# Feed-forward in chunks of 6, 8 and 8 hidden tiles, the down products of two chunks as 2x2 block products, and one more weight sum made by an accumulating transfer

## The chip, the cores and the metric

The kernel runs on one core of a Trainium2 chip, in one launch. The metric is the device time of one execution in microseconds (us). All arithmetic is on fp32 data.

## The reference

One layer of a hybrid encoder trunk runs over 512 prompt frames and 32 sample frames with the same weights (D_MODEL 1024, D_FF 2816, 544 columns of tokens in all):

```python
def swiglu(x, wg, wu, wd):
    return (jax.nn.silu(x @ wg) * (x @ wu)) @ wd
...
    x = x + 0.5 * swiglu(rms_norm(x, g_ffn1), w_ffn1_gate, w_ffn1_up, w_ffn1_down)
    y, st = hybrid_mixer(rms_norm(x, g_mix), pos, C, n, m, R, w_in, b_gates, g_gn_mlstm, g_gn_ret, w_out)
    x = x + y
    x = x + 0.5 * swiglu(rms_norm(x, g_ffn2), w_ffn2_gate, w_ffn2_up, w_ffn2_down)
```

`hybrid_mixer` projects with `w_in` (4104 columns), runs four mLSTM heads and four retention heads, and projects back with `w_out`. A last RMSNorm over the 1024 features gives the two outputs `y_prompt` and `y_sample`; the states go out too. The change touches the two feed-forward networks (FFN1 and FFN2) and their ends.

## The kernel before

The residual stream stays in SBUF transposed as `xT`: 8 tiles of 128 features by 544 tokens. An fp32 product is made of three passes of TensorE over split operands: `w_hi*x_hi + w_hi*x_lo + w_lo*x_hi`. ACT makes each `hi` by a copy that rounds, DVE each `lo` by subtracting. A matmul here is a 128x128 weight tile against 272 tokens, half of the 544.

**A feed-forward** has 22 hidden tiles of 128. The first four ("plain") are ordinary gate and up products over 8 k-tiles. The other 18 are made in "pairs" of two tiles, by a 2x2 block scheme of Winograd's kind (the features halved one way, the tokens the other): 7 block products in place of 8. A pair has a gate step (e=0, banks `dense[0]` and one of `core_banks`) and an up step (e=1). One step is 7 products `o` = 0 to 6 of 4 k-tiles by 3 passes: 84 matmuls. Products 0, 2, 4 and 6 use bank 0 of the step, 1 and 5 bank 1, 3 bank 2; products 0, 1 and 3 start a bank, and the others add to what is in it. So before the next product goes into a bank, its state is read out, where the output needs it apart: ACT copies products 0, 1, 2 and 4 into `kept` (`KEPT`, `copy_product` L1137), and DVE builds the gate and up values of the four quarters from these copies and the banks (`gate_first`, `gate_second`, `gate_third`, `up_first`, `up_second`, `up_third`, `up_last`). The product after a copy waits for `product_copied`.

The weights of the seven products are blocks of 128x512: 0, 1, 3, 4 and 5 are loaded by SyncE's queue. Blocks 1 and 4 then get a second quarter of the weights added by a transfer with accumulation that GpSimd (POOL) issues (`add_blocks` L2130). Block 2 is a sum that DVE makes of two blocks (`sum_t2`), block 6 likewise (`sum_t4` L1529, the addition at L1534). While step g runs, ACT and DVE prepare the `hi` (`block_to_hi` L1106) and the `lo` (`block_to_lo` L1536) of step g+1's blocks, each in the slot that the same product of step g has just left: `hi` of block o waits for `product_done` of product o.

The pairs come in two chunks, pairs 0 to 7 and 8 to 17 (`PAIRS`). The hidden tiles of a chunk (12, then 10) are then multiplied by `w_down` in ordinary products (`down` L779, `product` L614): 22 k-tiles by 8 output tiles by 3 passes by 2 token halves are 1056 matmuls for each feed-forward. DVE adds each finished tile to `xT` (L1798). In chunk 1 the squares of `xT` for the next norm follow on DVE, and POOL adds them up in SBUF (`add_square` L2120). The last tile of FFN2 goes out in two parts (`last_tile` L808), with the column sums (L836), the transposes (L845) and the scaling of the output (L1839) behind them.

The order on each engine is that of the code, written out by hand for five engines; semaphores are all that ties them together. SyncE's queue and POOL's queue are in order too.

Of the kernel before, what the change touches and what calls it, by code (L numbers as in the profile page):

```python
# [12 lines left out]
P = 128  # L13
# [31 lines left out]
def hybrid_trunk_step(nc, x_prompt, x_sample, state_mlstm_C, state_mlstm_n, state_mlstm_m, state_ret_R,  # L45
# [29 lines left out]
    U_DOWN = [[u + 2 * STD + 2 * DT * c for c in range(2)] for u in U_STD]  # L75
# [12 lines left out]
    LAST_COLS = [slice(2 * P, T), slice(0, 2 * P)]  # L88


    END_CHUNKS = [(2, 3, NC), (0,), (1,)]
    END_COLS = [slice(2 * P, T), slice(0, P), slice(P, 2 * P)]
    STEP_OF = {c: step for step, chunks in enumerate(END_CHUNKS) for c in chunks}
    DVE_COLS, ACT_COLS = slice(0, 5 * P), slice(5 * P, D)
    RAW = 4
# [6 lines left out]
    T_DOWN = [[t + 2 * STD + DT * c for c in range(2)] for t in T_STD]  # L102

    def down_unit(s):

        for n in range(2):
            for c in range(2):
                if U_DOWN[n][c] <= s < U_DOWN[n][c] + 2 * DT:
                    return n, c, s - U_DOWN[n][c]
        return None  # L110

    def k_tiles(s):

# [11 lines left out]
    NEGATED = (2, 6)  # L125
    KEPT = (0, 1, 2, 4)
# [8 lines left out]
    def units_before(n, c):  # L135

        return U_STD[n] + 2 * STD if c == 0 else U_DOWN[n][0] + 2 * DT

    with ExitStack() as ctx:
# [37 lines left out]
        rms_bias = sb("rms_bias", [P, NC + 1])  # L177
# [2091 lines left out]
```

## Time and profile before

| | before |
|---|---|
| median of 3 runs | 1064.79 us (1064.61 to 1065.61) |
| span of the profiled execution | 1063.2 us |
| its own time | 1063.2 us, 1.6 us under the median |
| PE (TensorE matmul) busy | 1055.5 us, 99% |
| DVE, ACT, POOL busy | 64%, 44%, 18% |
| granted TensorE clock | 9 tenths or more in each of 40 slices |

PE is busy nearly all of the span; a busy PE is one that has a matmul under way, and neighbouring matmuls overlap, so the duration of one is longer than the distance between two.

### The profile page before, as it was taken

How to read it: one execution, taken by the hardware profiler on the slowest of the kernel's cores; microseconds unless marked ns; L12 is line 12 of the kernel's file. 1: busy time of each engine (PE TensorE's matmuls, PEld its weight loads, DVE VectorE, ACT ScalarE, POOL GpSimd, SP SyncE). 2: the span in 40 equal slices, each digit the busy share in tenths (PEclk: the TensorE clock that was granted, in tenths of full speed). 3: DMA queues.
4: the chain of work that ended last, by engine and by line, in shares of the span. 5: the costliest groups of instructions: out<-in, count | busy, mean ns of one | idle time of the engine just before them, and what ended most of it. 6: DMA issues, size and time to landing. Idle time of an engine off the chain costs nothing.

```text
span 1063.2 us, 20510 instructions
## 1 busy us (share of the span) xinstructions
PE 1055.5 (99%) x8425; PEld 1052.1 (99%) x8425; DVE 684.2 (64%) x1170; ACT 465.7 (44%) x822; POOL 189.8 (18%) x169
## 2 busy tenths in 40 slices
PE   9999999999999999999999999999999999999997
PEld 8999999999999999999999999999999999999997
DVE  6997752367866676655655556598875236777555
ACT  6466641256652345433222224446664114666323
POOL 1122100112201211210332222212210002220111
PEclk9999999999999999999999999999999999999999
DMA  8589482479833377445454224547958328892422
GB/s 225 121 172 200 100 196 84 96 159 177 176 82 96 64 135 139 71 68 80 69 80 75 67 78 62 140 91 170 206 110 187 92 82 166 178 180 52 124 75 84
DMA packets 245493, 127.84 MB, mean 120 GB/s; under 512 B 9228, under 2 KB 243892, under 8 KB 245272
## 3 DMA queue, kind: packets, MB, share of 16 engines
q1 hardware_dynamic: 207032, 106.79, 41.6%
q0 software_dynamic: 38288, 19.72, 14.6%
q8 instruction: 67, 1.10, 0.4%
q14 instruction: 26, 0.21, 0.1%
q10 hardware_dynamic: 80, 0.02, 0.0%
HBM read 123.22 MB, written 3.29 MB: 119 GB/s over the span
## 4 chain that ended last, share of the span: by engine, by line
PE 98%; DMA 1%; DVE 0%; SPq 0%; issue 0%; ACT 0%
PE dense L623 52%; PE dense L768 31%; PE core_banks L768 5%; PE core_banks L623 3%; PE dense L691 1%; PE core_banks L928 1%; PE core_banks L943 1%; PE dense L824 1%; PE core_banks L946 1%; PE core_banks L918 1%; DMA x_tok<-in_x_prompt 1%; PE core_banks L955 0%; PE core_banks L912 0%; PE core_banks L914 0%; PE core_banks L805 0%; PE core_banks L666 0%
## 5 line engine op out<-in xcount | busy, mean ns | idle before, releaser
L1481 DVE TENSOR_TENSOR w_lo<-w_raw,w_hi 128x1024 fp32r<-128x1024 f32 (+2 forms) x118 | 131.7, 1133 | 55.1 <-ACT w_hi L1068 55.0
L1068 ACT ACTIVATE w_hi<-w_raw 128x1024 fp32r<-128x1024 f32 (+2 forms) x118 | 105.2, 904 | 89.3 <-PE dense L623 81.4
L623 PE MATMUL dense<-h_hi,w_hi 128*128 128x272 f32 x684 | 142.5, 290 | 0.0
L623 PE MATMUL dense<-xg_hi,w_hi 128*128 128x272 f32 x672 | 142.2, 293 | 0.0
L623 PE MATMUL dense<-h_lo,w_hi 128*128 128x272 f32 x684 | 141.1, 287 | 0.0
L623 PE MATMUL dense<-h_hi,w_lo 128*128 128x272 f32 x684 | 140.9, 287 | 0.0
L623 PE MATMUL dense<-xg_lo,w_hi 128*128 128x272 f32 x672 | 138.9, 288 | 0.0
L623 PE MATMUL dense<-xg_hi,w_lo 128*128 128x272 f32 x672 | 138.8, 287 | 0.0
L768 PE MATMUL dense<-x_op_hi,w_lo 128*128 128x272 f32 x432 | 124.6, 289 | 0.0
L768 PE MATMUL dense<-x_op_hi,w_hi 128*128 128x272 f32 x432 | 124.5, 288 | 0.0
L768 PE MATMUL dense<-x_late_hi,w_lo 128*128 128x272 f32 x432 | 124.5, 288 | 0.0
L768 PE MATMUL dense<-x_late_hi,w_hi 128*128 128x272 f32 x432 | 124.3, 288 | 0.0
L768 PE MATMUL dense<-x_late_lo,w_hi 128*128 128x272 f32 x432 | 124.2, 287 | 0.0
L768 PE MATMUL dense<-x_op_lo,w_hi 128*128 128x272 f32 x432 | 124.0, 287 | 0.0
L1539 DVE TENSOR_TENSOR w_lo<-w_src,w_hi 128x512 fp32r<-128x512 f32 x126 | 85.9, 690 | 50.1 <-ACT w_hi L1120 49.9
L1798 DVE SCALAR_TENSOR_TENSOR xT<-dense,xT 128x544 f32<-128x544 f32 x38 | 27.5, 724 | 135.4 <-PE dense L623 135.4
L623 PEld LDWEIGHTS dense<-h_lo,w_hi 128*128 128x128 f32 x684 | 107.8, 188 | 0.0
L623 PEld LDWEIGHTS dense<-h_hi,w_lo 128*128 128x128 f32 x684 | 106.8, 188 | 0.0
L623 PEld LDWEIGHTS dense<-h_hi,w_hi 128*128 128x128 f32 x684 | 106.7, 188 | 0.1
L623 PEld LDWEIGHTS dense<-xg_lo,w_hi 128*128 128x128 f32 x672 | 105.8, 188 | 0.0
L623 PEld LDWEIGHTS dense<-xg_hi,w_lo 128*128 128x128 f32 x672 | 105.1, 188 | 0.0
L623 PEld LDWEIGHTS dense<-xg_hi,w_hi 128*128 128x128 f32 x672 | 104.7, 188 | 0.2
(341 smaller groups left out, 2212.1 us busy)
## 6 DMA issues: line engine op xcount, KB each, us to landing
w_raw<-in_w_ffn_up SPq DMA_DIRECT2D x91, 256.0 KB, 3.6
w_src<-in_w_ffn_gate SPq DMA_DIRECT2D x90, 256.0 KB, 4.6
w_raw<-in_w_in SPq DMA_DIRECT2D x32, 512.0 KB, 8.9
w_raw<-in_w_ffn_down SPq DMA_DIRECT2D x32, 384.0 KB, 4.0
w_raw<-in_w_ffn_down SPq DMA_DIRECT2D x32, 320.0 KB, 3.5
w_src<-in_w_ffn_gate POOLq DMA_DIRECT2D x36, 256.0 KB, 5.2
w_raw<-in_w_ffn_up POOLq DMA_DIRECT2D x36, 256.0 KB, 5.8
w_raw<-in_w_out SPq DMA_DIRECT2D x8, 512.0 KB, 3.9
```

The source lines that it names most:

```text
L623: last = nc.tensor.matmul(out[:, half, 0:TH], w[:, s % 4, k, :], x(kt)[:, half * TH:(half + 1) * TH], start=start and n == 0 and m == 0, s ...
L691: last = nc.tensor.matmul(bank_of(u)[:, half, 0:TH], w[:, u, k, :], x(k)[:, half * TH:(half + 1) * TH], start=part == "hh" and k == 0, sto ...
L768: last = nc.tensor.matmul(banks[BANK[o]], w[:, k, :], x[:, k, :], start=o in OPENS and k == 0 and m == 0, stop=k == KH - 1 and m == 2, ski ...
L824: last = nc.tensor.matmul(bank_of(t)[:, part, 0:cols.stop - cols.start], w[:, (s + u) % 4, kt - u * split, :], x[:, kt, cols], start=kt == ...
L918: nc.tensor.matmul(X[:, 3, CH[c]], p(h, 1, CH[c]), p(h, 0, CH[c]), start=True, stop=True)
L928: last = nc.tensor.matmul(X[:, b, o * V1:(o + 1) * V1], k_tail[:, c, :], v_tok[:, c, :], start=True, stop=True)
L943: last = nc.tensor.matmul(out, score_tail[:, block], v_tok[:, c, :], start=True, stop=c == 0)
L946: last = nc.tensor.matmul(out, sum_ident[:, block], state, start=False, stop=True)
L1068: nc.scalar.activation(w_hi[:, s % 4, 0:k_tiles(s), :], raw, ACT.Copy).then_inc(w_hi_ready, 1)
L1481: nc.vector.tensor_tensor(w_lo[:, s % 4, 0:nk, :], w_raw[:, s % RAW, 0:nk, :], w_hi[:, s % 4, 0:nk, :].bitcast(F32), ALU.subtract).then_in ...
L1539: nc.vector.tensor_tensor(block_of(w_lo, n, o), source(p % 2, o), block_of(w_hi, n, o).bitcast(F32), ALU.subtract)\
L1798: nc.vector.scalar_tensor_tensor(x, halves(tile), factor, x, ALU.mult, ALU.add).then_inc(evicted, 1)
```

## The change

The hidden tiles are now worked in three chunks: 6 (the four plain ones and pairs 0 and 1), 8 and 8 tiles. Only the first chunk's down products are still ordinary (`down(n)`, 6 k-tiles). Those of the other two chunks are made in four steps each, `down_pair(n, c, d)` for d = 0 to 3: a step makes two output tiles over eight hidden tiles, again by 7 block products of 4 k-tiles by 3 passes, with weight blocks of `w_down` that are loaded, summed and split as those of a pair. There are now 26 steps for each feed-forward. Their moving operands are seven combinations of four hidden half tiles, which DVE and ACT prepare for each group of two tiles: four sums (`sum_h`), seven `hi` (`h_to_hi`) and seven `lo` (`h_to_lo`) of 128x272 each. DVE adds every one of the 7 products to `xT` (`take_down`).

Two things change for the pair steps. ACT copies products 0, 1 and 2 only; of product 4 DVE itself reads the bank (`gate_second`, `up_second`), and product 6 waits for that. And DVE's `sum_t4` is gone: a third accumulating transfer of POOL's adds a quarter of the weights to block 2, once block 2's `lo` is made (`add_last_block`), and that is block 6.

At the end of a feed-forward the squares of tiles 1 to 5 are made by ACT (`square_end`) and added by transfers from SBUF to SBUF with accumulation, one after the other (`add_end_square`); those of the last two tiles are added by DVE. The end of FFN2 is rewritten for tiles that come out in pairs.

```diff
-    PAIRS = (range(0, 8), range(8, 18))
-    FC, F0 = (12, FT - 12), (0, 12)
...
+    PAIRS = (range(0, 2), range(2, 10), range(10, 18))
+    FC, F0 = (STD + 2, 8, 8), (0, STD + 2, STD + 10)
...
-    KEPT = (0, 1, 2, 4)
+    COPIED = (0, 1, 2)
+
+
+    DOWNS = DT // 2
+    STEPS = NP + 2 * DOWNS
...
+    FIRST_ORDER = (0, 1, 3, 2, 4, 5, 6)
+    LAST_ORDER = (0, 1, 3, 2, 5, 4, 6)
...
                     if o == 6:
-                        pe.wait_ge(product_copied, 4 * P_ + 4)
+                        if e == 0:
+                            pe.wait_ge(pair_gate_made, 3 * Q + 2)
+                        else:
+                            pe.wait_ge(pair_up_taken, 3 * Q + 2)
...
+            def down_pair(n, c, d):
...
+                    pe.wait_ge(down_taken, BLOCKS * D + 2)
+                    pe.wait_ge(block_lo, BLOCKS * g + 6)
+                    part(5, range(KH // 2))
+                    pe.wait_ge(down_taken, BLOCKS * D + 4)
+                    pe.wait_ge(h_op_lo_ready, lo_made(n, k, 4))
+                    part(4, range(KH)).then_inc(product_done, 1)
...
+                for rank, o in enumerate(order_of(g)):
...
+                    before = {2: 0, 4: 2, 5: 1, 6: 4}
+                    if o in before:
+                        pe.wait_ge(down_taken, BLOCKS * D + order_of(g).index(before[o]) + 1)
...
             def gate_second(n, p):
-                dve.wait_ge(product_copied, 4 * pair_index(n, p) + 4)
-                nc.vector.tensor_tensor(pair_gate[1][:, TH:T], kept[:, 0, 3, :], kept[:, 0, 1, :], ALU.add).then_inc(pair_gate_made, 1)
+                dve.wait_ge(product_done, done_by(step_of_pair(n, p), 4))
+                dve.wait_ge(product_copied, 3 * pair_index(n, p) + 2)
+                out = pair_gate[1][:, TH:T]
+                nc.vector.tensor_tensor(out, pair_banks(0)[0], out, ALU.subtract).then_inc(pair_gate_made, 1)
...
-            def sum_t4(n, p):
...
+            def take_down(n, c, d, o):
...
+                dve.wait_ge(product_done, done_by(g, o))
...
+                x = xT[:, 2 * d + m, half * TH:(half + 1) * TH]
+                nc.vector.scalar_tensor_tensor(x, pair_banks(g % 2)[BANK[o]], factor, x, ALU.mult, ALU.add).then_inc(down_taken, 1)
...
+            def add_end_square(n, j):
+
+                pool.wait_ge(end_squared, DT * n + j + 1)
+                if j > 1:
+                    pool.wait_ge(end_landed, 16 * ((DT - 3) * n + j - 1))
+                nc.gpsimd.dma_start(sq_sum[:, :], sq[:, :], accum_op=ALU.add).then_inc(end_landed, 16)
...
+            def add_last_block(g, quarter):
+
+                e = g % 2
+                pool.wait_ge(block_lo, BLOCKS * g + 3)
+                nc.gpsimd.dma_start(source(e, 6), quarter(1, 0), accum_op=ALU.add).then_inc(block_summed[e][6], 16)
```

In DVE's program, around products 4 and 5 of a gate step of FFN1, the order before was this. `w_lo` is a weight block's `lo` for the next step, `sq` and `rstd` hold the gate values, `h_lo` the split of hidden values, L1589 is `gate_second`.

```order
L1539 TENSOR_TENSOR w_lo<-w_raw,w_hi 128x512 [waits block_hi]
L1585 TENSOR_TENSOR sq<-core_banks,kept 128x272 [waits product_copied,product_done,pair_h_made]
L1637 TENSOR_TENSOR h_lo<-sum_ident,h_hi 128x544 [waits pair_h_hi]
L1539 TENSOR_TENSOR w_lo<-w_raw,w_hi 128x512 [waits block_hi]
L1589 TENSOR_TENSOR rstd<-kept 128x272 [waits product_copied]
L1539 TENSOR_TENSOR w_lo<-w_raw,w_hi 128x512 [waits block_hi]
L1593 SCALAR_TENSOR_TENSOR rstd<-dense,kept 128x272 [waits product_done]
L1637 TENSOR_TENSOR h_lo<-h_f,h_hi 128x544 [waits pair_h_hi]
```

At the same place of the changed program (L1717 is `block_to_lo`, L1759 `h_to_lo`, L1792 `gate_second`):

```order
L1717 TENSOR_TENSOR w_lo<-w_raw,w_hi 128x512 [waits block_hi]
L1759 TENSOR_TENSOR h_op<-h_raw,h_op 128x272 [waits h_op_hi_ready]
L1786 TENSOR_TENSOR sq<-core_banks,sq 128x272 [waits product_copied,product_done]
L1717 TENSOR_TENSOR w_lo<-w_raw,w_hi 128x512 [waits block_hi]
L1759 TENSOR_TENSOR h_op<-h_raw,h_op 128x272 [waits h_summed,h_op_hi_ready]
L1792 TENSOR_TENSOR rstd<-dense,rstd 128x272 [waits product_copied,product_done]
L1717 TENSOR_TENSOR w_lo<-w_raw,w_hi 128x512 [waits block_hi]
L1759 TENSOR_TENSOR h_op<-h_raw,h_op 128x272 [waits h_op_hi_ready]
L1798 TENSOR_TENSOR rstd<-dense,rstd 128x272 [waits product_copied,product_done]
L1717 TENSOR_TENSOR w_lo<-w_raw,w_hi 128x512 [waits block_hi]
```

`gate_second` stands behind the `lo` of block 4 and an operand's `lo` now as it stood behind the `lo` of block 4 before, but it reads the bank, and it needs product 4 itself where it needed ACT's copy.

In PE's program the first matmul of product 6 of a gate step waited before for the block's `lo` and for ACT's copy:

```order
L768 MATMUL dense<-x_late_hi,w_hi 128x272
L768 MATMUL dense<-x_late_lo,w_hi 128x272
L768 MATMUL dense<-x_late_hi,w_lo 128x272
L768 MATMUL dense<-x_late_hi,w_hi 128x272 [waits block_lo,product_copied]
L768 MATMUL dense<-x_late_lo,w_hi 128x272
```

In the changed program it waits for the `lo` and for DVE's `gate_second`:

```order
L853 MATMUL dense<-x_late_hi,w_hi 128x272
L853 MATMUL dense<-x_late_lo,w_hi 128x272
L853 MATMUL dense<-x_late_hi,w_lo 128x272
L853 MATMUL dense<-x_late_hi,w_hi 128x272 [waits block_lo,pair_gate_made]
L853 MATMUL dense<-x_late_lo,w_hi 128x272
```

Nothing else stands between product 5 and product 6 in either.

The third place is DVE's program at the start of a chunk's down products. Before, it was this (L1637 and L1624 finish the last pair's hidden values, L1481 is the `lo` of a `w_down` tile, L1798 the addition of a finished tile to `xT`):

```order
L1624 TENSOR_TENSOR sum_ident<-sum_ident,rstd 128x544 [waits pair_gate_silu,pair_up_taken]
L1630 SCALAR_TENSOR_TENSOR h_f<-dense,sq 128x272 [waits pair_gate_silu,product_done]
L1637 TENSOR_TENSOR h_lo<-sum_ident,h_hi 128x544 [waits pair_h_hi]
L1637 TENSOR_TENSOR h_lo<-h_f,h_hi 128x544 [waits pair_h_hi]
L1481 TENSOR_TENSOR w_lo<-w_raw,w_hi 128x768 [waits w_hi_ready] x2
L1798 SCALAR_TENSOR_TENSOR xT<-dense,xT 128x544 [waits unit_done]
L1481 TENSOR_TENSOR w_lo<-w_raw,w_hi 128x768 [waits w_hi_ready] x2
L1798 SCALAR_TENSOR_TENSOR xT<-dense,xT 128x544 [waits unit_done]
```

In the changed program the first down step, d=0, begins so (L1747 and L1756 or L1759 make the last group's operands, L1712 is `sum_t2`, L1846 `take_down`):

```order
L1846 SCALAR_TENSOR_TENSOR xT<-dense,xT 128x272 [waits product_done]
L1759 TENSOR_TENSOR h_op<-h_raw,h_op 128x272 [waits h_summed,h_op_hi_ready]
L1846 SCALAR_TENSOR_TENSOR xT<-dense,xT 128x272 [waits product_done]
L1846 SCALAR_TENSOR_TENSOR xT<-core_banks,xT 128x272 [waits down_taken,product_done]
L1759 TENSOR_TENSOR h_op<-h_raw,h_op 128x272 [waits h_summed,h_op_hi_ready]
L1717 TENSOR_TENSOR w_lo<-w_src,w_hi 128x512 [waits block_hi]
L1712 TENSOR_TENSOR w_raw<-w_raw 128x512 [waits block_lo,block_loaded1_5,block_summed1_1]
L1756 SCALAR_TENSOR_TENSOR h_op<-h_raw,h_op 128x272 [waits h_op_hi_ready]
L1717 TENSOR_TENSOR w_lo<-w_raw,w_hi 128x512 [waits block_hi]
L1846 SCALAR_TENSOR_TENSOR xT<-dense,xT 128x272 [waits product_done]
L1717 TENSOR_TENSOR w_lo<-w_raw,w_hi 128x512 [waits block_hi] x3
L1846 SCALAR_TENSOR_TENSOR xT<-dense,xT 128x272 [waits down_taken,product_done]
```

Between two evictions stand now the last group's `lo` operands and the weight blocks of the next step, and an eviction comes for each block product.

## Rows read from the trace of the kernel before

**Rows 1.** The page's head, its engines, and the chain that ended last

```profile
span 1063.2 us, 20510 instructions
...
PE 1055.5 (99%) x8425; PEld 1052.1 (99%) x8425; DVE 684.2 (64%) x1170; ACT 465.7 (44%) x822; POOL 189.8 (18%) x169
...
PE 98%; DMA 1%; DVE 0%; SPq 0%; issue 0%; ACT 0%
```

**Rows 2.** PE's waits: what for, us in total, times, longest

```profile
PE core_banks L866 <- POOL ones L2111: 1.1, 1, 1.1
```

**Rows 3.** Windows, a pair stretch, then a down stretch: length, busy time of each engine (count), clock, DMA share, GB/s

```profile
740.00:760.00 20.00, 20.00 (x162) 20.00 (x161) 17.84 (x33) 12.36 (x25) 5.12 (x4) 1.00 1.01 218
820.00:840.00 20.00, 20.00 (x161) 20.00 (x161) 4.92 (x6) 3.47 (x5) 0.00 (x0) 1.00 0.53 130
```

**Rows 4.** Groups of instructions: the costliest of the down products, busy, mean ns, idle before

```profile
L623 PE MATMUL dense<-h_hi,w_hi 128*128 128x272 f32 x684 | 142.5, 290 | 0.0
```

**Rows 5.** Timeline, gate step: product 4's last, product 6's first matmul, and ACT and DVE between

```profile
956.31 0.29 PE L768 MATMUL dense<-x_late_hi,w_lo 128*128 128x272 f32 x1
...
956.63 0.40 ACT L1141 ACTIVATE kept<-dense 128x272 f32<-128x272 f32 x1 [0.26 <-PE dense L768]
...
956.93 0.63 ACT L1120 ACTIVATE w_hi<-w_raw 128x512 fp32r<-128x512 f32 x1
...
957.59 0.69 DVE L1539 TENSOR_TENSOR w_lo<-w_raw,w_hi 128x512 fp32r<-128x512 f32 x1
...
957.94 0.28 PE L768 MATMUL dense<-x_late_hi,w_hi 128*128 128x272 f32 x1
```

**Rows 6.** Timeline, DVE's queue in the up step behind it

```profile
968.72 0.43 DVE L1610 TENSOR_TENSOR h_f<-h_f,sq 128x272 f32<-128x272 f32 x1
969.08 0.43 DVE L1614 TENSOR_TENSOR sum_ident<-kept 128x272 f32<-128x272 f32 x1
969.43 0.68 DVE L1539 TENSOR_TENSOR w_lo<-w_src,w_hi 128x512 fp32r<-128x512 f32 x1
970.03 0.43 DVE L1618 SCALAR_TENSOR_TENSOR sum_ident<-dense,kept 128x272 f32<-128x272 f32 x1
```

**Rows 7.** Timeline, ACT's copy of the same product in two steps that follow each other

```profile
961.15 0.40 ACT L1141 ACTIVATE kept<-dense 128x272 f32<-128x272 f32 x1 [0.49 <-PE dense L768]
...
971.67 0.40 ACT L1141 ACTIVATE kept<-dense 128x272 f32<-128x272 f32 x1 [0.81 <-PE dense L768]
```

**Rows 8.** Timeline, PE's restart behind a DVE result

```profile
1052.80 0.46 DVE L1812 TENSOR_TENSOR sq<-sq,sum_ident 128x288 f32<-128x288 f32 x1
...
1053.35 0.35 PE L836 MATMUL dense<-ones,sq 128*128 128x1 f32 x2
```

**Rows 9.** One line's transfers: L2138, accumulating, 256 KB, into block 4

```profile
L2138 POOL DMA_DIRECT2D w_src<-in_w_ffn_gate x18: 1270/1279/1296, 37.4 to 951.0; - x18
...
DMA to landing us min/median/max: 4.5/5.3/8.3
```

**Rows 10.** One line's transfers: L2207, plain, 272 KB, from POOL's queue

```profile
L2207 POOL DMA_DIRECT2D row_all<-row_copy x3: 547/591/614, 410.2 to 449.0; - x3
...
DMA to landing us min/median/max: 3.6/3.7/8.3
```

**Rows 11.** Groups of instructions by form, of the seams: busy, mean ns, idle before

```profile
L1486 DVE SCALAR_TENSOR_TENSOR xg_lo<-xT,gains,xg_hi 128x544 fp32r<-128x544 f32 x24 | 27.6, 1168 | 4.5 <-ACT xg_hi L1080 4.1
L1624 DVE TENSOR_TENSOR sum_ident<-sum_ident,rstd 128x544 f32<-128x544 f32 x18 | 13.0, 720 | 0.1
L1080 ACT ACTIVATE xg_hi<-xT,gains 128x544 fp32r<-128x544 f32 x24 | 17.5, 746 | 60.2 <-DVE xT L1798 59.6 <-DVE xT L1848 0.6
L1074 ACT ACTIVATE sq<-xT 128x544 f32<-128x544 f32 x8 | 5.2, 646 | 1.5 <-POOL sum_ident L2128 1.5
L2128 POOL TENSOR_TENSOR sum_ident<-sum_ident,sq 128x544 f32<-128x544 f32 x22 | 31.6, 1436 | 121.5 <-DVE sq L1786 89.6 <-ACT sq L1074 31.9
```

**Rows 12.** The end: the last product matmul, the last scaling, and the last window

```profile
1056.11 0.28 PE L824 MATMUL dense<-h_hi,w_lo 128*128 128x256 f32 x1
...
1059.06 0.55 DVE L1839 TENSOR_SCALAR y_tok<-y_tok,rms_tok 128x640 f32<-128x640 f32 x1
...
1058.00:1063.00 5.00, 0.33 (x2) 0.14 (x1) 1.54 (x6) 1.45 (x4) 0.00 (x0) 0.68 0.82 317
```

**Rows 13.** The page's DMA queues: packets, MB, share of 16 engines

```profile
q1 hardware_dynamic: 207032, 106.79, 41.6%
q0 software_dynamic: 38288, 19.72, 14.6%
```

More of the change, by code:

```diff
@@ L85, in hybrid_trunk_step @@
     X_BY_DVE = [piece for piece in X_PIECES if piece != X_BY_ACT]
[L88 to L93, printed above, removed]
+    HALF_COLS = [slice(0, TH), slice(TH, T)]
+    END_CHUNKS = [(0, 1), (2, 3, NC)]
+    END_COLS = [slice(0, 2 * P), slice(2 * P, T)]
     DVE_COLS, ACT_COLS = slice(0, 5 * P), slice(5 * P, D)
+    Y_PARTS = (2, 2, 2, 2, 1)
     RAW = 4
@@ L761, in pair @@
                     if p == 0:
                         pe.wait_ge(x_op_ready, BLOCKS * n + o + 1)
[L763 to L764 removed]
+                    pe.wait_ge(block_lo, BLOCKS * g + o + 1)
                     x_hi, x_lo = x_op(x_op_hi, x_late_hi, o), x_op(x_op_lo, x_late_lo, o)
[L766 to L769 removed]
@@ L832, in column_sums @@
-            def column_sums(out, source, chunks):
-                for c in chunks:
-                    n = P if c < NC else TS
-                    last = nc.tensor.matmul(out[0:n, c:c + 1], source[:, CH[c]], ones[:, 0:1], start=True, stop=True)
-                return last
-            def turn_last(step):
-                pe.wait_ge(out_taken, DT - 1 if step == 2 else DT - 2)
-                pe.wait_ge(x_gained, DT + step)
-                j = DT - 1
-                for c in END_CHUNKS[step]:
-                    last = nc.tensor.transpose(last_turn(c), x_gain[:, j % 2, CH[c]], ident[:, :])
+                    nc.tensor.transpose(X[:, 2 + j % 2, CH[c]], x_gain[:, j % 2, CH[c]], ident[:, :])
@@ L859, in turn_dummies @@
+                for c in END_CHUNKS[step]:
+                    last = nc.tensor.matmul(final_sum(c), sq_last[:, 0, CH[c]], ones[:, 0:1], start=True, stop=True)
+                last.then_inc(final_sums, 1)
             def turn_dummies(n):
@@ new lines, in ffn, with sum_t2 @@
+                pair(n, 0, 1)
+                up_last(n, 1, NP // 2 * n)
+                first_to_lo(n, STD + 1)
+                first_to_lo(n, STD)
+                down(n)
+                block_to_lo(n, STEPS * n + STEP_DOWN + 1, BLOCKS - 1)
+                for c in (1, 2):
+                    for p in PAIRS[c]:
+                        pair(n, c, p)
+                    for d in range(DOWNS):
+                        down_pair(n, c, d)
+            def sum_t2(g):
+                e = g % 2
+                dve.wait_ge(block_summed[e][1], 16 * (g // 2 + 1))
+                dve.wait_ge(block_loaded[e][5], 16 * (g // 2 + 1))
+                if g > 1:
+                    dve.wait_ge(block_lo, BLOCKS * (g - 1))
+                nc.vector.tensor_tensor(source(e, 2), source(e, 1), source(e, 5), ALU.add).then_inc(pair_summed, 1)
@@ L1666, in pair @@
                     if o == 0:
-                        if e == 0 and p - 2 in PAIRS[c]:
+                        if deferred and e == 0:
                             up_last(n, p - 1, Q - 1)
-                        if more:
-                            sum_t2(n, p + 1)
-                    if o == 3 and more:
-                        sum_t4(n, p + 1)
+                        if follows_blocks(g):
+                            sum_t2(g + 1)
+                    if deferred:
+                        for h_o in ((), (1,), (2,), (4, 5), (), (), ())[o] if e == 0 else ():
+                            sum_h(n, k, h_o)
+                        for h_o in (((), (), (), (), (0,), (1,), (3,)), ((2,), (4,), (5,), (6,), (), (), ()))[e][o]:
+                            h_to_lo(n, k, h_o)
```

1143 lines of the change are left out of this document (664 added, 479 removed).

## The prediction

> **What bounds the kernel now.** I read the page's head and its chain first. PE is busy 1055.5 of 1063.2 us, and 98% of the chain that ended last is PE [rows 1]. PE's own waits are four in all and the longest is 1.1 us, at the start of the mixer [rows 2]. So nothing can be won but matmuls, and every wait put in front of a matmul costs its full length. The windows show what lies beside PE: in a pair stretch DVE is busy 17.84 of 20 us, ACT 12.36, and the DMA engines' share is 1.01; in a down stretch DVE is busy only 4.92 us and the share is 0.53 [rows 3]. The change takes matmuls out of the idle stretches and turns them into more of the crowded kind.
>
> **1. The matmuls.** The h rows are three kinds of 684 [rows 4], with the 60 of the last tile 2112 down matmuls for both networks. A down stretch has 161 in 20 us, 124.2 ns each [rows 3]. A pair step of 84 lasts from 961.15 to 971.67, 10.52 us, 125.2 ns each [rows 7]. After the change 2 x 6 x 8 x 3 x 2 = 576 stay plain, and 2 x 8 x 84 = 1344 are block products. −2112 x 0.1242 + 576 x 0.1242 + 1344 x 0.1252 = −262.3 + 71.5 + 168.3 = **−22.5 us**. This is the whole gain: the kept copies of product 4 and `sum_t4` leave engines that PE didn't wait for.
>
> **2. Product 6 of a pair step.** Before, product 4 ends at 956.60 and product 6 starts at 957.94 [rows 5]: 1.34 us, product 5's length, without a gap, since ACT's copy (0.40 us, from 956.63) was long done. Now product 6 waits for `gate_second` or `up_second`, and DVE does it behind the next step's block 4 `lo`, which itself waits for a `hi` that ACT can start only when product 4 is done. From the end of product 4: hand-over 0.03, `hi` 0.63, hand-over 0.03 [rows 5], so the `lo` starts at 0.69. DVE's queue then moves by 0.60 for a 512-wide `lo` (969.43 to 970.03) and 0.36 for a 272-wide operation (968.72 to 969.08) [rows 6]; in a gate step an `h_to_lo` is next, in an up step `up_first_gated`, both 272 wide. So the sum starts at 0.69 + 0.60 + 0.36 = 1.65 and ends 0.43 later, at 2.08. PE starts about 0.09 after DVE's end (1053.26 to 1053.35) [rows 8]: 2.17 against 1.34, **0.83 us of idle PE**. It occurs in the 16 pairs of the last two chunks of each network, 32 steps, less 0.36 in the four that have no operand's `lo` between (the first gate step of a chunk). Pairs 0 and 1 have no such `lo` ahead. 28 x 0.83 + 4 x 0.47 = **+25.1 us**. Below, 0.75 a step if the hand-overs are shorter (+22); above, 0.95 if DVE comes late to the `lo` (+30), as its queue is nearly full. Nothing hides it, since PE has no other work in its queue.
>
> **3. The first down step of a chunk (4 of them).** Here the last group's hidden values are only finished after the last pair step. I walk DVE's queue from the end of that step, t = 0. PE does the old k-tiles of products 0, 1 and 3 first (27 matmuls), then the last ones (9), product 2 (12), half of 5 (6): product 4 could start after 54 matmuls, at 6.6. It waits for `take_down` of product 2. Take 3 can start at 4.65 (36 matmuls and the pipeline); behind it stand an `h_lo` (0.36), a weight `lo` (0.60), `sum_t2` (0.60), an `h_lo` (0.36), a weight `lo` (0.60), by the pitches of [rows 6], so take 2 starts at 7.5 and PE at 8.05. That is 1.5 us, **+6** (3 to 8).
>
> **4. Block 6 behind that step.** In the same queue the `lo` of block 2 of the next step comes at 8.5 and ends at 9.2. Only then POOL may issue the transfer that makes block 6. An accumulating 256 KB transfer of this kind lands 5.3 us after its issue (4.5 to 8.3) [rows 9]: 14.5. `hi` 0.63 and `lo` 0.60 with hand-overs follow, to 15.8, and only behind this `lo` stands take 0 of the next step, 0.43. PE's product 2 of that step waits for take 0: 16.3 against 14.8. **+6** for four (3 to 10, with the landing). In the steps after that the loop from block 2's `lo` to product 2 of the next step adds up to 1.4 + 0.1 + 5.3 + 0.7 + 0.6 + 0.4 + 0.2 = 8.7 us, where 72 matmuls give 9.0: hidden, by 0.3 us. A landing later than the median shows, so I put **+1** (0 to 5) for late ones.
>
> **5. FFN1 to mixer.** The five transfers of squares run one after the other; each link is a square on ACT (0.65), a hand-over (0.1) and a landing. No row has an accumulating 272 KB transfer within SBUF; a plain one from POOL's queue takes 3.7 [rows 10], an accumulating one 5.3 [rows 9]. I take 4.7 between them, nearer to the one that accumulates: 5.45 a link. POOL's queue lets the first go about 0.9 us before step d=2, so the fifth lands at −0.9 + 4.7 + 4 x 5.45 = 25.6 after that step's start, 15.1 after the last step's, which itself ends at 10.5. Behind it stand a square 0.65, `add_end` 0.72, `normed_lo` 1.17, take 0.43, `normed_hi` 0.75, `normed_lo` 1.17, `add_end` 0.72, with hand-overs some 6 us [rows 11], where PE waits for the sums. They are ready at 21, the first mixer product at 21.9. By the matmuls alone it would start at 10.5 + 32 x 0.124 + 0.6 = 15.1. **+7** (3 to 10). Before, POOL's additions took 1.44 each [rows 11].
>
> **6. The end of FFN2.** Product 6 of the last step stands behind `sum_last(0)`, which needs the fifth landing: PE goes on at 15.7 where 72 matmuls and the transposes end at 9.6: +6. Then the tail. Before, 3.2 us lie between the last product's end (1056.39) and the end of the last scaling (1059.61) [rows 12]; now an addition, three reads of transposes and all five scalings stand behind it, 5.3 us as I add them, +2. **+8** (4 to 12).
>
> **Sum.** −22.5 + 25.1 + 6 + 6 + 1 + 7 + 8 = +30.6, 1063.2 + 30.6 = 1093.8. The profiled execution is 1.6 us under the median of 1064.8, so against the median 1095.4; I say **1096**. All terms at their low ends give 1077, all at the high ones 1118.
>
> **Rivals.**
> *(a) The DMA engines become the bound* (0.14). POOL's queue took 14.6% of 1063.2 us for 19.72 MB [rows 13], and 72 weight transfers make nearly all of that: 2.1 us of all 16 engines each; SyncE's took 41.6% for 106.79 MB, 1.09 us for 256 KB. A step had 5 x 1.09 + 2 x 2.1 = 9.7 us and gets 11.8, more than the 10.5 of its matmuls and about 0.5 more than a step with its stalls. Against it: the times of packets include their waiting for each other. For it: the 1.01 of [rows 3]. Over 52 steps, half of the full 0.5, 14 us: about 1110, in the range.
> *(b) Part of the waits are not there* (0.08): DVE or ACT are given earlier starts than I walked, the squares' transfers land in 3.7 us. With terms 3 to 6 at half and term 2 at 0.6 us a step (19): 1063 − 22.5 + 19 + 14 + 1.6 = 1076; 1066 to 1077.
> *(c) The other side: product 6 doesn't wait* (0.08). One mechanism would do it: if `gate_second` ran as soon as product 4 is done, 0.03 + 0.43 + 0.09 = 0.55, well before 1.34, term 2 is nothing and the kernel takes 1070; with the seams at their low ends (3 + 3 + 3 + 4) 1057. It decides where the stall falls under 22.5/32 = 0.7 us a step with the seams free. For it speaks only that DVE's order could have been read wrongly; the order shows the `lo` ahead of it.
> *(d) The clock* (0.08). In the last window, where PE has 0.33 us of work in 5, the granted clock is 0.68, and it is 1.00 in both busy stretches [rows 12, 3]. In the seams PE now idles some us at a time. If it falls to the lower level behind each of the two seams, 50 matmuls at twice 0.124 cost 6 us: 1102, in the range. The Trainium skill (TensorE: Matmul & The Clock Gate, Part 1: The HAM clock gate) says that the array is throttled to half its clock unless recent activity releases it. The trace agrees in so far as the clock sank where PE stopped.
>
> **How the numbers follow.** Forecast 0.62, (a) 0.14, (b) 0.08, (c) 0.08, (d) 0.08. From 1076 to 1118 lie the forecast, (d), most of (a) and the top of (b). Under 0.2% (2 us) a run can't be told from no change. Only (c) without most of the seams is faster, 0.07, or the same, 0.02; the rest is slower, 0.91.
>
> **What would show it.** Term 1: 192 fewer matmuls (their records may be a few short). Term 2: PE's waits name DVE's `gate_second` (L1792) and `up_second` (L1816) about 16 times each, at 0.7 to 0.9 us; this one decides, and if they are absent I am wrong by 25 us. Terms 3 and 4: eight waits for `take_down` (L1846) of 1 to 2 us, one pair to each chunk. Term 5: one wait of some 6 us for the sums of squares ahead of the mixer, with transfers of 272 KB that land 4 to 5 us after their issue. Term 6: the same ahead of the last product 6, and a tail of 5 us. (a): waits that name DMAs of weights, a share above 1.0 in down steps; (d): a granted clock under 1.0 behind a seam. It would be wrong, too, if landings of the third transfer stretch well over 5.3 us, since the loop of term 4 has 0.3 us to spare: each us more costs up to 40 us over the steps, which is the largest single risk above the range.

## The result, and the profile after

The changed kernel takes 1149.97 us (median of 4 runs, 1143.43 to 1153.29) against 1064.74 us before: 1.079 times as long, 95% interval 1.075 to 1.082. The prediction was 1096 us with a range of 1076 to 1118. The sign was right, the size was not: +85 us where +31 were forecast.

The page's head after the change, then PE's longest waits (what for, us in total, times, longest):

```profile
span 1150.2 us, 20921 instructions
...
PE 1058.8 (92%) x8229; PEld 1041.4 (91%) x8229; DVE 759.7 (66%) x1441; ACT 509.6 (44%) x943; POOL 286.5 (25%) x246
...
PE 71%; DMA 13%; DVE 7%; ACT 4%; issue 4%; SPq 0%; POOL 0%; DVEq 0%; ACTq 0%; POOLq 0%
```

```profile
PE dense L853 <- DVE xT L1846: 16.1, 8, 2.9
PE dense L853 <- DVE rstd L1792: 14.2, 18, 2.1
PE dense L739 <- DVE xg_lo L1673: 11.7, 1, 11.7
PE dense L739 <- DVE w_hi L1663: 11.6, 1, 11.6
PE dense L853 <- DVE h_raw L1816: 11.3, 16, 0.7
PE dense L853 <- ACT sq L1293: 5.0, 2, 2.8
PE core_banks L977 <- ACT x_gain L1411: 2.8, 2, 1.4
PE core_banks L986 <- DVE y_tok L1688: 1.9, 1, 1.9
...
PE core_banks L774 <- DVE sum_ident L1993: 1.3, 1, 1.3
...
PE dense L986 <- ACT x_gain L1451: 0.4, 1, 0.4
```

PE was 99% busy and 98% of the chain [rows 1]; it is now 92% and 71%. To see where the time went, the root of the norm sums is a mark that both kernels have once behind FFN1 and once ahead of FFN2. Before (first and last start):

```profile
L1089 ACT ACTIVATE rstd<-core_banks,eps x2: 715/716/718, 387.2 to 685.7; 128x544 f32<-128x544 f32 x2
```

After:

```profile
L1233 ACT ACTIVATE rstd<-core_banks,eps x2: 713/716/718, 441.0 to 739.4; 128x544 f32<-128x544 f32 x2
```

| | before | after |
|---|---|---|
| FFN1, to the root | 387.2 | 441.0 (+53.8) |
| mixer | 298.5 | 298.4 |
| FFN2, to the end | 377.5 | 410.8 (+33.3) |

So nothing happened in the mixer, and FFN1 lost 20 us more than FFN2. The windows say where: first a pair stretch, then the first two down steps of FFN1's last chunk, then two at the seam to the mixer (columns as in [rows 3]).

```profile
200.00:220.00 20.00, 18.59 (x146) 18.15 (x145) 16.56 (x36) 12.38 (x29) 6.66 (x6) 1.00 1.00 196
360.00:380.00 20.00, 15.70 (x111) 15.26 (x110) 14.20 (x32) 8.35 (x17) 5.13 (x4) 0.92 0.78 142
400.00:420.00 20.00, 8.44 (x63) 8.22 (x62) 3.73 (x10) 2.93 (x6) 2.88 (x5) 0.77 0.63 83
420.00:440.00 20.00, 7.04 (x28) 6.16 (x27) 5.25 (x7) 4.08 (x5) 3.47 (x14) 0.59 0.66 153
```

Where PE had been idle for some us, the granted clock sank too: 0.59 at the seam means that most of that window's records ran at the lower of the two levels.

In a pair step the predicted wait stands as it was walked. The timeline of one gate step: the last matmul of product 4, ACT's and DVE's operations behind it, the last matmul of product 5 and the first two of product 6; the next step's product 6 follows.

```profile
902.28 0.29 PE L853 MATMUL dense<-x_late_hi,w_lo 128*128 128x272 f32 x1
...
902.66 0.63 ACT L1265 ACTIVATE w_hi<-w_raw 128x512 fp32r<-128x512 f32 x1 [0.55 <-PE dense L853]
...
903.20 0.74 ACT L1301 ACTIVATE h_op<-h_raw 128x272 fp32r<-128x272 f32 x2
903.33 0.69 DVE L1717 TENSOR_TENSOR w_lo<-w_raw,w_hi 128x512 fp32r<-128x512 f32 x1
...
903.78 0.29 PE L853 MATMUL dense<-x_late_hi,w_lo 128*128 128x272 f32 x1
903.94 0.43 DVE L1759 TENSOR_TENSOR h_op<-h_raw,h_op 128x272 fp32r<-128x272 f32 x1
...
904.29 0.43 DVE L1792 TENSOR_TENSOR rstd<-dense,rstd 128x272 f32<-128x272 f32 x1
...
904.78 0.40 PE L853 MATMUL dense<-x_late_hi,w_hi 128*128 128x272 f32 x1 [0.71 <-DVE rstd L1792]
...
905.01 0.29 PE L853 MATMUL dense<-x_late_lo,w_hi 128*128 128x272 f32 x1
...
916.28 0.39 PE L853 MATMUL dense<-x_late_hi,w_hi 128*128 128x272 f32 x1 [0.71 <-DVE h_raw L1816]
```

The block's `lo`, the operand's `lo` and the sum follow at 0.61 and 0.35 us, and PE starts 0.06 us after the sum's end. From one product 6 to the next are 11.50 us where a step took 10.52 [rows 7]: 0.98 us. 0.71 of them are named as a wait. This wait is counted from the end of the matmul before, which lasts 0.29 us where the distance between two is 0.125, so product 6 starts 0.87 us late; and its second matmul comes 0.23 us behind the first, another 0.10.

At the seam, ACT and POOL stand still for 17 us, and DVE behind them for 13.8, until a transfer of squares lands. SyncE's queue (SPq) has issued three 512 KB loads of `w_in` ahead of it:

```profile
398.99 0.99 SPq L624 DMA_DIRECT2D w_raw<-in_w_in  x2
...
400.03 3.65 SPq L624 DMA_DIRECT2D w_raw<-in_w_in  x1
400.62 0.85 POOL L2398 DMA_DIRECT2D sum_ident<-sq  x1
...
417.50 0.66 ACT L1404 ACTIVATE sq<-xT 128x544 f32<-128x544 f32 x1 [17.04 <-DMA sum_ident<-sq]
418.06 0.33 ACT L1194 ACTIVATE w_hi<-w_gates 128x32 fp32r<-128x32 f32 x2
...
418.42 0.29 DVE L1663 TENSOR_TENSOR w_hi<-w_gates,w_hi 128x32 fp32r<-128x32 f32 x2 [13.76 <-ACT w_hi L1194]
418.45 0.86 POOL L2398 DMA_DIRECT2D sum_ident<-sq  x1 [16.97 <-ACT sq L1404]
418.75 0.37 SPq L624 DMA_DIRECT2D w_raw<-in_w_in  x1
418.77 0.82 PE L739 MATMUL dense<-xg_hi,w_hi 128*128 128x272 f32 x2 [11.56 <-DVE w_hi L1663]
```

This is the fourth of FFN1's five transfers and takes 16.9 us; the fifth, issued at 418.45, takes 15.5. The landings of all ten such transfers (L2398), and of the third accumulating weight transfer (L2412), min, median, max:

```profile
DMA to landing us min/median/max: 3.3/3.3/16.9
...
DMA to landing us min/median/max: 4.4/5.7/8.0
```

### The profile page after: what moved, and what is told of

It is laid out like the page before. It is cut to its first block, busy times and chain, and to the rows that moved or that the text cites. A ratio compares the mean times of both kernels' runs of the same rounds, so it can differ in the third digit from the quotient of the medians.

```text
span 1150.2 us, 20921 instructions
## 1 busy us (share of the span) xinstructions
PE 1058.8 (92%) x8229; PEld 1041.4 (91%) x8229; DVE 759.7 (66%) x1441; ACT 509.6 (44%) x943; POOL 286.5 (25%) x246
## 4 chain that ended last, share of the span: by engine, by line
PE 71%; DMA 13%; DVE 7%; ACT 4%; issue 4%; SPq 0%; POOL 0%; DVEq 0%; ACTq 0%; POOLq 0%
PE dense L729 29%; PE dense L853 27%; PE core_banks L853 6%; DMA sum_ident<-sq 3%; DMA w_raw<-in_w_ffn_up 3%; DMA w_raw<-in_w_ffn_down 3%; PE core_banks L729 3%; DMA w_src<-in_w_ffn_gate 3%; ACT w_hi L1265 2%; DVE w_lo L1717 2%; PE dense L799 1%; PE core_banks L1080 1%; PE core_banks L1065 1%; DMA x_tok<-in_x_prompt 1%; PE core_banks L1055 1%
## 5 line engine op out<-in xcount | busy, mean ns | idle before, releaser
L1717 DVE TENSOR_TENSOR w_lo<-w_raw,w_hi 128x512 fp32r<-128x512 f32 x182 | 123.8, 688 | 79.2 <-ACT w_hi L1265 77.0
L1265 ACT ACTIVATE w_hi<-w_raw 128x512 fp32r<-128x512 f32 x182 | 112.8, 629 | 134.8 <-DMA w_raw<-in_w_ffn_up 47.2
L1265 ACT ACTIVATE w_hi<-w_src 128x512 fp32r<-128x512 f32 x182 | 112.5, 627 | 135.1 <-DMA w_src<-in_w_ffn_gate 49.5
L1717 DVE TENSOR_TENSOR w_lo<-w_src,w_hi 128x512 fp32r<-128x512 f32 x182 | 124.4, 689 | 65.3 <-ACT w_hi L1265 62.7
L853 PE MATMUL dense<-h_op,w_hi 128*128 128x272 f32 x768 | 150.1, 294 | 16.1 <-DVE xT L1846 16.1
L853 PE MATMUL dense<-x_late_hi,w_hi 128*128 128x272 f32 x432 | 128.2, 297 | 26.3 <-DVE rstd L1792 14.2
L853 PEld LDWEIGHTS dense<-h_op,w_hi 128*128 128x128 f32 x768 | 121.8, 191 | 18.5 <-DVE xT L1846 18.3
L1668 DVE TENSOR_TENSOR w_lo<-w_raw,w_hi 128x1024 fp32r<-128x1024 f32 (+1 forms) x70 | 87.5, 1250 | 43.5 <-ACT w_hi L1211 43.3
L853 PE MATMUL dense<-h_op,w_lo 128*128 128x272 f32 x384 | 112.1, 292 | 0.0
L853 PEld LDWEIGHTS dense<-x_late_hi,w_hi 128*128 128x128 f32 x432 | 81.1, 188 | 34.0 <-DVE rstd L1792 18.2
L853 PEld LDWEIGHTS dense<-x_op_hi,w_hi 128*128 128x128 f32 x432 | 81.5, 189 | 8.9 <-ACT sq L1293 5.7
```

Source lines behind the costliest of these rows:

```text
L853: last = nc.tensor.matmul(out, w[:, k, :], x, start=o in OPENS and k == 0 and m == 0, stop=k == KH - 1 and m == 2, skip_group_check=o not ...
L1265: nc.scalar.activation(block_of(w_hi, n, o), source(e, o), ACT.Copy).then_inc(block_hi, 1)
L1668: nc.vector.tensor_tensor(w_lo[:, s % 4, 0:nk, :], w_raw[:, s % RAW, 0:nk, :], w_hi[:, s % 4, 0:nk, :].bitcast(F32), ALU.subtract).then_in ...
L1717: nc.vector.tensor_tensor(block_of(w_lo, n, o), source(g % 2, o), block_of(w_hi, n, o).bitcast(F32), ALU.subtract)\
```

## The experiments

Each kernel was timed beside the kernel before (1064.9 to 1065.1 us in these rounds). The changed kernel took 1149.97.

| edit | us | ratio to before, 95% |
|---|---|---|
| sums first | 1143.77 | 1.072 to 1.075 |
| squares by POOL | 1132.15 | 1.061 to 1.064 |
| late w_in | 1139.84 | 1.067 to 1.075 |
| block 6 by DVE | 1132.49 | 1.062 to 1.065 |
| sums first, block 6 by DVE | 1105.38 | 1.034 to 1.041 |
| sums first, squares, early take | 1123.70 | 1.050 to 1.057 |
| all four | 1095.22 | 1.024 to 1.032 |
| and w_in split last | 1092.89 | 1.021 to 1.029 |
| and better DVE order | 1074.03 | 1.007 to 1.010 |
| and root first | 1069.88 | 1.004 to 1.006 |
| better order, block 6 by transfer | 1132.15 | 1.060 to 1.066 |
| before, sum from the bank | 1101.89 | 1.033 to 1.036 |
| before, block 6 by transfer | 1095.13 | 1.027 to 1.033 |
| before, both | 1101.05 | 1.033 to 1.036 |

**Sums first.** DVE does the sum for product 6 ahead of the next block's `lo`.

```diff
                         if e == 0:
                             gate_first(n, p, Q)
+                            gate_second(n, p)
                         else:
                             up_first(n, p)
-                    if o == 5:
-                        if e == 0:
-                            gate_second(n, p)
-                        else:
+                            up_first_gated(p, Q)
                             up_second(n, p)
...
-                    if e and o == 4:
-                        up_first_gated(p, Q)
```

> DVE does gate_second and up_second ahead of the next step's block 4 lo; nothing else is changed. Theory A (each pair step idles at product 6 only because DVE's sum stands behind that lo): the 32 waits of PE for these sums, 0.7 us each with a restart of 0.1, fall away and a step goes back from 11.5 to 10.5 us, 28 to 31 us in all, so about 1120 us. Rival B (the DMA engines, at a share of 0.95 to 1.0 in these stretches, set the step's length anyway): the waits turn into waits for weight blocks, the step stays above 11 us, gain under 12 us, about 1140.

The waits at product 6 of a steady step are gone (two, in the first gate step of each network, are left), but 6 us are all that came of it. The new waits are at product 2, for ACT's copy of product 0, and those for `take_down` rose from 16.1 to 20.2 us:

```profile
PE dense L853 <- DVE xT L1846: 20.2, 10, 3.9
...
PE dense L853 <- ACT h_raw L1293: 9.4, 13, 1.6
PE dense L853 <- ACT sq L1293: 4.7, 4, 2.0
PE dense L853 <- DVE rstd L1792: 4.1, 2, 2.1
```

The gain is as small as rival B had it, but its sign, waits for weight blocks, isn't there: PE waits for ACT's copies. Another limit of almost the same length stood behind the first. Which one, the next runs tell.

**Squares by POOL's addition.** `add_end_square` adds with an instruction.

```diff
-                nc.gpsimd.dma_start(sq_sum[:, :], sq[:, :], accum_op=ALU.add).then_inc(end_landed, 16)
+                nc.gpsimd.tensor_tensor(sq_sum[:, :], sq_sum[:, :], sq[:, :], ALU.add).then_inc(end_landed, 16)
```

> The five squares of each network's end are added by POOL's own tensor addition in place of the accumulating transfer. Theory A (two of the transfers ahead of the mixer take 16.9 us because they lie behind the 512 KB loads of w_in in the DMA engines): the two idle stretches of PE ahead of the mixer, 11.6 and 11.7 us, go down to under 3 us together, and with the clock kept up the kernel gains 22 to 28 us, about 1124. Rival B (the mixer's weights themselves land late): PE waits for w_in instead, gain under 10 us, about 1142.

It gave 18 us, less than theory A's 22 to 28. The first of the two long waits is gone, the second is 6.0 us; there ACT waits 9.88 us for the landing of a `w_in` tile, which stands in its program ahead of the last squares. So theory A holds for the greater part and rival B for the rest.

**The squares' transfers kept, w_in held back.** SyncE waits for the last of them ahead of three loads; its queue is in order, so all that it issues later waits too.

```diff
                     sp.wait_ge(block_lo, BLOCKS * STEP_LAST + (2, BLOCKS, 6, 6)[s % RAW])
+                    sp.wait_ge(end_landed, 16 * (DT - 3))
```

> The transfers of squares are kept, but the first three loads of w_in are held back until the last of them has landed. Theory A: all five transfers of FFN1 land in 3.3 to 3.6 us instead of two in 16.9; PE's wait moves to the weights of the mixer, which now come some 10 us after the squares; gain 5 to 15 us, 1135 to 1145. Rival C (the transfer is slow for a reason of its own, as what ACT and DVE write or read beside it): two still take above 10 us and the kernel gets slower, 1160.

```profile
DMA to landing us min/median/max: 3.3/3.3/3.6
```

All ten transfers now land in 3.3 to 3.6 us, and PE has one wait of 15.2 us left at this place instead of two of 11.6 and 11.7. The 16.9 and 15.5 us were time beside what SyncE's queue had under way, the 512 KB loads of `w_in` first of all; the transfer has no slowness of its own. This is shown by the one edit.

**Block 6 by DVE,** as before the change, in all steps.

```diff
                     .then_inc(block_lo, 1)
+                if o == 2 and summed_by_dve(g):
+                    sum_t4(g)
...
+                nc.vector.tensor_tensor(source(e, 6), source(e, 2), source(e, 3), ALU.add).then_inc(block_summed[e][6], 16)
...
             def add_last_block(g, quarter):
 
+                if summed_by_dve(g):
+                    return
```

> Block 6 is summed by DVE again, as before the change, in all 52 steps; no third accumulating transfer. Theory A (the loop over block 6's transfer costs where it starts late): product 2 of the second down step, 2.4 to 3.2 us four times with a slower clock behind it, and product 2 at the start of chunk 1, 2.1 and 2.8 us, lose their waits; product 6's waits stay at 0.7 us; gain 14 to 22 us, about 1132. Rival B (DVE is too full for the sum): 0.6 us more on DVE for each step shows up as longer waits at product 6, gain under 5 or a loss.

It gave 17 us. The waits for `take_down` fell from 16.1 to 7.2 us and those for ACT's `sq` are gone, but those at `gate_second` rose from 14.2 to 23.0: the theory holds, and a part of rival B too.

**Both,** sums first and block 6 by DVE:

> Both edits at once: gate_second and up_second ahead of the next block's lo, and block 6 summed by DVE. Alone they gave 6 and 17 us. Theory A (two loops bind a pair step one behind the other, DVE's order at product 6 and the landing of block 6's transfer, so that either edit alone only brings the other out): together they give much more than 23 us, the waits at product 6 (40 us of PE in the run with DVE's block 6) go nearly whole, about 1098 us, pair steps of 10.5 to 10.7 us. Rival B (DMA share of 1.0 binds whatever is done): with a third fewer accumulating transfers this rival too allows a gain, but it would show as waits for loads; and rival D (DVE is full: 17.9 of 20 us) leaves waits at products 2 or 6, about 1115.

Together they gave 44.6 us, where the two alone gave 6 and 17. That is what two limits behind each other look like.

**The other repairs on top.** Three runs follow. The first has the sums first, the squares by POOL and an early take: `take_down` of product 2 goes ahead of `sum_t2` in a chunk's first down step. The second adds block 6 by DVE ("all four"). In the third ACT and DVE also split the first `w_in` tile behind the last squares. The edit of the early take:

```diff
                     next_lo(n, g - 1, 6)
+                    take_down(n, c, d, 2)
                     sum_t2(g + 1)
                     h_to_lo(n, k, 6)
                     next_lo(n, g, 0)
-                    take_down(n, c, d, 2)
```

> DVE's sums first, squares added by POOL, the fourth down eviction of a chunk's first down step ahead of sum_t2 and two lo; the third accumulating transfer stays. Theory A: 6 + 18 + 4 us off 1150 (the parts are at different places), about 1121 us, with the waits of product 2 for ACT's copy still there. If the third transfer were not what binds the pair steps, 1095 to 1105.

> The same with block 6 summed by DVE. Theory A: 1098 (both loops gone) less 18 for the squares and 4 to 6 for the early take: about 1075 us, still above the kernel before. Rival D (DVE full) about 1090.

> As the run before, and ACT and DVE split the first w_in tile behind the last squares and normalised tiles instead of ahead of them. Theory A (what is left of the seam, 6 us of idle PE and some us at half clock, is ACT and DVE standing behind the late w_in load): 4 to 8 us less than the run before, about 1069 us. If the late load itself is what PE needs, under 2 us.

They took 1123.7 us (3 more than expected), 1095.2 (20 more than expected) and 1092.9. The last is 2 us less, at the edge of what can be told, where 4 to 8 were expected: PE now waits 5.3 us for DVE's rows a little later. The early take didn't pay: PE's wait moved from `take_down` of product 2 to that of product 4, 2.0 us each.

**One part alone in the kernel before.** These are the cleanest, since nothing else of the change is there. First the sum from the bank: ACT doesn't copy product 4, and product 6 waits for DVE. Then block 6 by a third accumulating transfer. Then both.

```diff
-    KEPT = (0, 1, 2, 4)
+    KEPT = (0, 1, 2)
...
-                        pe.wait_ge(product_copied, 4 * P_ + 4)
+                        pe.wait_ge(*((second_taken, Q + 1) if e else (pair_gate_made, 3 * Q + 2)))
```

> The kernel before with one part of the change alone: product 4 isn't copied by ACT, DVE reads its bank behind the next block 4's lo, and product 6 waits for DVE. Theory A: an up step idles for 0.85 us at product 6 (one 272-wide operation between), a gate step for 0.5, with 0.1 for a restart each; 16 steps of either kind, so 20 to 25 us more, about 1087 us. Rival: the wait is hidden in the kernel before, whose DVE has fewer operations, 1065 to 1070.

> The kernel before with the other part alone: block 6 is made by a third accumulating transfer instead of by DVE. Theory A (the transfer's landing, 5.7 us after its issue, closes a loop of about one step's length through hi of block 6, ACT's copy of product 0 and product 2): steps of 10.5 us become 10.8 to 11.3, 10 to 25 us in all, 1075 to 1090 us, with waits of PE for ACT's copies. Rival (the loop has room at DVE's lower load): 1065 to 1068.

> Both parts in the kernel before. Theory A: the idle time at product 6 gives block 6's transfer the time that it lacks, so the two do not add: as the first part alone or up to 6 us more, about 1090 us. If they were independent: the sum of both.

The first costs 37 us where 20 to 25 were expected:

```profile
PE dense L769 <- DVE rstd L1590: 14.4, 18, 3.4
PE dense L769 <- DVE sum_ident L1616: 9.9, 14, 0.7
```

They name 24.3 us. The 14 waits of an up step are 0.7 us each and those of a steady gate step 0.5, as walked; a named wait of 0.71 costs 0.98 in the step, as above. What the expectation lacked is a wait of 3.4 us in the first gate step of each network, together 7 of the 12 us by which it missed. The transfer alone costs 30 us, and its waits are those that came up in the first experiment,

```profile
PE dense L768 <- ACT kept L1141: 18.8, 12, 4.1
```

and both together cost 36, no more than the first: the idle time at product 6 gives the transfer the time that it lacks, and the waits for ACT's copies fall to 3.9 us. This is the coupling of theory A without the down steps.

**A better order on DVE.** On top of all repairs, `take_down` of product 4 goes ahead of two weight `lo`, `gate_second` ahead of the operands' `lo`, and in a network's first gate step both sums ahead of the weight `lo`.

```diff
+                    take_down(n, c, d, 4)
                     next_lo(n, g, 2)
                     next_lo(n, g, 3)
-                    take_down(n, c, d, 4)
```

> The changed kernel with all four repairs and a better order on DVE: take_down of product 4 ahead of two lo in a chunk's first down step, gate_second ahead of the operands' lo, and ahead of two lo in a network's first gate step. Theory A: the waits for DVE that are left (2.0 us at four chunks, 0.4 us with restart 0.5 in 14 gate steps, 2.8 us twice) go, 18 us less than 1093: about 1075. Rival D (DVE, at 17.4 of 20 us, has no room, and a wait taken away here comes back later): above 1086.

It took 1074.03 us, as expected. DVE is busy 17.6 of 20 us in a pair stretch, about what it was in the kernel before [rows 3], and it isn't too full if the operation that PE waits for comes first.

**Root first,** at the mixer's start; and, from the better order, **back to the transfer** for block 6.

```diff
+            root(1)
             split_hi(0, U_IN + 1, 0)
-            root(1)
             split_hi(0, U_IN + 2, 0)
```

> As the run with the better order, and at the mixer's start ACT takes the root of the sums before it splits the second w_in tile (whose load lands late), DVE inverts it before its part of that split. Theory A: the root comes 4 us earlier, PE's wait of 5.4 us for DVE's rows shrinks to 1 to 2, 1070 us. If the late load of that tile is what PE needs next: no gain, 1073 to 1074.

> The run with the better order, but block 6 by the third accumulating transfer as in the changed kernel. Theory A (the transfer's loop is longer than a step of 10.5 us and now sets it): 30 us over 1074 as in the kernel before (1095 against 1065), that is 1100 to 1108 us. If the transfer cost only what it added to full DVE queues: under 1085.

The root comes 3.8 us earlier and PE's wait falls from 5.4 to 2.2 us: 1069.88, the best of the changed kernels, and 0.5% over the kernel before. The transfer costs 58 us there, where 26 to 34 were expected from the 30 us that it cost in the kernel before. That kernel has 36 such transfers and this one 52: 0.8 and 1.1 us for each. PE's waits for ACT's copies are 25.0 us in all, and those for `take_down` 18.4, up to 4.8 each, where the run without the transfer has 0.5. In the timeline of this last run its loop is seen whole: the issue, ACT's `hi` of block 6 as it lands, ACT's copy of product 0 behind that, PE's product 2.

```profile
168.57 1.27 POOL L2410 DMA_DIRECT2D w_src<-in_w_ffn_gate  x1 [2.61 <-DVE w_lo L1717]
...
174.88 0.63 ACT L1265 ACTIVATE w_hi<-w_src 128x512 fp32r<-128x512 f32 x1 [2.76 <-DMA w_src<-in_w_ffn_gate]
175.42 0.38 ACT L1293 ACTIVATE sq<-dense 128x272 f32<-128x272 f32 x1
...
175.85 0.40 PE L853 MATMUL dense<-x_op_hi,w_hi 128*128 128x272 f32 x1 [0.24 <-ACT sq L1293]
```

POOL issues it when block 2's `lo` is made, which waits for product 2 of the step before, and product 2 of the next step waits for the copy that stands behind the landing. Round this loop are 6.3 us of landing and some 5 us of work, and a step has 10.5. From 156.58 to 202.81 us POOL issues it every 11.56 us in the mean. The DMA engines' share in such stretches is 0.94 to 1.03; in two of the run with the better order and without the transfer, 0.86 and 0.90.

## Why the prediction was wrong

The sum forecast +31 us and +85 came. The step that failed most is term 5, the price of a transfer's landing at the seam to the mixer: where 7 us were put down, the named waits alone are 24.6. The other terms missed by 5 us or less each, and term 1, the gain, held.

*Term 1 holds as far as it can be seen.* The profile has 196 fewer matmul records, and in the last changed kernel, where few waits are left, FFN1 ends 1.6 us before it did in the kernel before (root at 385.6 against 387.2).

*Term 2, product 6,* was the right wait at the right places (18 and 16 times for the two sums) with the right walk: from product 4's end (902.57) to product 6 are 2.21 us, where I had 2.17. The size was 0.98 us for a step and not 0.83, since the second matmul behind the restart comes 0.10 us later too, which I had left out: 30 us, not 25. "Pairs 0 and 1 have no such `lo` ahead" was wrong: the first gate step of each network waits 2.06 us for `gate_second`, which stands behind four operands' `lo` of 1.3 us and three of weights.

*Term 3* came as walked: the wait is 1.4 us each time, 1.65 with the late start and the matmul behind it.

*Term 4* failed in size: 2.8, 2.9, 2.1 and 2.7 us and not 1.5, for the transfer took 6.0 to 6.8 us there where I put the old median of 5.3. In three of these four stretches the granted clock was 0.91; behind the shortest of the waits it was 1.00. I had written that the loop of the steps behind it is hidden by 0.3 us, and named each us of later landing as the largest risk. I had not looked for the same loop in the pair steps, where it is just hidden behind the stall of term 2. In the changed kernel itself it costs at chunk starts only: product 2 of pair 2 waits 2.1 and 2.8 us for ACT, behind block 6, whose transfer took 8.0 and 7.9 us there.

*Term 5* is the step that failed most, "a landing, I take 4.7". The price was even too high for three of the five transfers, and the last two took 16.9 and 15.5 us. The error was to take a landing as a property of the transfer. Three 512 KB loads of `w_in` are issued from 399.0 to 400.0, 0.6 to 1.6 us before the fourth transfer, and a fourth load 0.3 us after the fifth transfer. I walked only POOL's queue, not what SyncE's queue puts into the same DMA engines. FFN1's 20 us more than FFN2's are this seam: 24.6 us of named waits (11.6, 11.7 and 1.3) and a low clock, against 5.1 us of waits at FFN2's end and 2.8 us of a longer tail.

*Term 6* came out near its 8 us, by luck. The 6 us for the fifth landing aren't there: beside no such loads all five transfers of FFN2 land in 3.3 us. In their place stand waits of 2.8, 1.9 and 0.4 us for the transposes' operands, which I hadn't walked. The tail behind the last product is 6.0 us where it was 3.2, +2.8 for the +2 forecast.

*The balance.* Of the 54 us missed, 17.6 are longer waits at the seam, 5 are in term 2, 5 in term 4, 4.9 are the waits of pair 2 and 4.1 those of the first gate steps. The other 17 or so weren't taken apart; a part of them is the clock, 0.978 in the mean where it was 0.998.

*The rivals.* (a) isn't what happened in the changed kernel: the share is 1.00 in pair stretches, but the step's length is explained by PE's waits for DVE, and in the kernel before the share was 1.01 while PE was busy all the time [rows 3]. It may have a part once DVE's waits are away, in the run with the transfer in a good order (+58 us). Whether there the DMA engines' load or the length of the loop binds, the runs don't separate, for taking the transfer out shortens both. (b) and (c) fell. (d) was right as an addition: mean clock 0.978. The Trainium skill (TensorE: Matmul & The Clock Gate, Part 1: The HAM clock gate) has an array throttled to half unless recent activity releases it, and the seam's 0.59 agrees.

*What stays open.* The last changed kernel has 22 us less of matmuls and is 5 us slower. Its mixer takes 301.1 us (2.6 more) and FFN2 382.8 (5.3 more), with 5.0 us of waits at the very end. In the run with the better order a steady pair step is still 10.8 to 10.9 us from product 6 to product 6, 0.3 to 0.4 over the old one, though hardly a wait is named in it: some 11 us for 32 steps. The trace shows where they are. It is product 6 still, in a gap too short to be listed as a wait:

```profile
159.03 0.43 DVE L1829 TENSOR_TENSOR h_raw<-dense,h_raw 128x272 f32<-128x272 f32 x1
159.09 0.29 PE L857 MATMUL dense<-x_late_hi,w_lo 128*128 128x272 f32 x1
...
159.52 0.39 PE L857 MATMUL dense<-x_late_hi,w_hi 128*128 128x272 f32 x1
159.75 0.29 PE L857 MATMUL dense<-x_late_lo,w_hi 128*128 128x272 f32 x1
```

`up_second` ends at 159.46 and product 6 starts 0.06 us later, 0.43 us behind the matmul before where 0.125 would be steady; the next one comes 0.10 us late. In a gate step (148.29 to 148.58) the start is 0.17 us late. So the sum from the bank, term 2's dependence, takes about half of what term 1 brings even in the best order tried. The rest of the 5 us, in the mixer and at the end, wasn't taken apart.

## What to carry to other kernels

A wait that is removed pays only up to the next loop of about the same length; so sum each loop that closes once per step (result, slot, load, copy, result), also the ones that look hidden by little, and compare them. Where an in-order engine makes both the thing PE waits for and things for the next step, the first comes first: order alone was worth 19 us here. A transfer's landing is priced with all that is issued into the same DMA engines ahead of it, by whichever queue; a short transfer on the critical path doesn't belong behind a prefetch.

## What was not expected of the hardware

- An accumulating transfer of 272 KB within SBUF lands 3.3 us after its issue beside no large load, sooner than the plain 272 KB transfer of [rows 10] with 3.7, and 16.9 us after it behind three 512 KB loads.
- A named wait of 0.71 us lengthens a step by 0.98: the first matmul behind the wait starts 0.87 us late, since the wait is counted from the end of the one before, and the second another 0.10.
- One accumulating transfer of 256 KB more for each step cost 30 us over 36 steps in one kernel and 58 over 52 in another, though its own landing, 5.6 and 5.9 us in the median, was nearly the same.
